# A new order of work at layer ends and at the start of two mixers of a transformer kernel

## Reference

```python
def swiglu(x, w13, w2):
    gate, up = jnp.split(x @ w13, 2, axis=-1)
    return (jax.nn.silu(gate) * up) @ w2
...
    idx_score = jnp.einsum('bqh,bqhk->bqk', wib, jax.nn.relu(dots))
...
    _, sel = lax.top_k(idx_score, topk)
...
    q = (rms_norm(cq, q_norm_g) @ w_uq).reshape(B, S, MLA_HEADS, MLA_NOPE + MLA_ROPE)
    kv = (rms_norm(ckv, kv_norm_g) @ w_ukv).reshape(B, S, MLA_HEADS, MLA_NOPE + MLA_V)
```

## Time and profile before

| | |
|---|---|
| Median of 3 runs | 2679.49 us (2677.05 to 2681.64) |
| The profiled execution | 2682.68 us, of which the span from first to last instruction is 2680.9 us |
| Mean granted TensorE clock | 0.971 |
| Busy share of the span: PE, PE weight load, DVE, ACT, POOL | 94%, 79%, 57%, 44%, 15% |
| DMA | 417.04 MB, 155 GB/s read from HBM over the span |
| Transfers of weights | 1 MB each, 48.1% of the time of 16 engines |

### The profile page before, as it was taken

The page is one execution under the profiler, slowest core; times in us unless marked ns, Lnnn a source line. Parts: engine busy times, 40 slices in busy tenths (PEclk is TensorE's granted clock), DMA queues, the critical chain, the costliest instruction groups (busy, mean ns, idle before and its releaser), DMA issues. The chain is left out here.

```text
span 2680.9 us, 32692 instructions
## 1 busy us (share of the span) xinstructions
PE 2527.9 (94%) x13229; PEld 2128.9 (79%) x13229; DVE 1524.4 (57%) x2152; ACT 1188.2 (44%) x1492; POOL 395.3 (15%) x466
## 2 busy tenths in 40 slices
PE   8998999999999999999789999998999987987998
PEld 6887878888888788888777888887778776886897
DVE  5546564464455544645455455456576565985455
ACT  4534454444444444444454444443444454333343
POOL 0001210000001000000220000002289112760000
PEclk9998999999999999999899999999999988988999
DMA  7554335555542555555135555554355531334453
GB/s 236 183 177 142 126 126 189 188 173 188 189 139 99 168 188 186 171 187 170 55 126 174 187 177 181 187 170 126 102 166 188 180 104 43 115 101 141 151 188 134
DMA packets 314967, 417.04 MB, mean 156 GB/s; under 512 B 18762, under 2 KB 273091, under 8 KB 314819
## 3 DMA queue, kind: packets, MB, share of 16 engines
q1 hardware_dynamic: 314818, 414.96, 48.1%
HBM read 413.87 MB, written 1.05 MB: 155 GB/s over the span
## 5 line engine op out<-in xcount | busy, mean ns | idle before, releaser
L456 DVE TENSOR_TENSOR wlo<-raw,whi 128x2048 fp32r<-128x2048 f32 (+3 forms) x402 | 919.7, 2293 | 640.3 <-ACT whi L448 639.4
L448 ACT ACTIVATE whi<-raw 128x2048 fp32r<-128x2048 f32 (+3 forms) x402 | 747.3, 1867 | 444.5 <-DMA raw<-in_ffn_w_dram 395.1
L569 PE MATMUL ps<-whi,xh 128*128 128x512 f32 (+4 forms) x2056 | 789.1, 384 | 25.7 <-DVE wlo L456 16.2
L570 PE MATMUL ps<-wlo,xh 128*128 128x512 f32 (+4 forms) x2056 | 777.5, 378 | 0.0
L571 PE MATMUL ps<-whi,xl 128*128 128x512 f32 (+4 forms) x2056 | 776.7, 378 | 0.0
L569 PEld LDWEIGHTS ps<-whi,xh 128*128 128x128 f32 x2056 | 397.7, 193 | 102.5 <-issue 23.3
L571 PEld LDWEIGHTS ps<-whi,xl 128*128 128x128 f32 x2056 | 397.2, 193 | 68.6
L570 PEld LDWEIGHTS ps<-wlo,xh 128*128 128x128 f32 x2056 | 398.2, 194 | 65.0
L569 PE MATMUL ps<-whi,oh 128*128 128x512 f32 x960 | 387.8, 404 | 6.0 <-DVE ol L1677 2.8
L571 PE MATMUL ps<-whi,ol 128*128 128x512 f32 x960 | 376.4, 392 | 0.0
L570 PE MATMUL ps<-wlo,oh 128*128 128x512 f32 x960 | 375.4, 391 | 0.0
(11 more groups left out here) (296 smaller groups left out, 2369.7 us busy)
## 6 DMA issues: line engine op xcount, KB each, us to landing
raw<-in_ffn_w_dram SPq DMA_DIRECT2D x352, 512.0 KB, 4.8
raw<-in_ffn_w_dram SPq DMA_DIRECT2D x88, 1024.0 KB, 5.0
raw<-in_w_ff_dram SPq DMA_DIRECT2D x32, 1024.0 KB, 5.3
raw<-in_w_out_dram SPq DMA_DIRECT2D x20, 1024.0 KB, 4.9
raw<-in_w_in_dram SPq DMA_DIRECT2D x20, 1024.0 KB, 5.2
raw<-in_dsa_w_in_dram SPq DMA_DIRECT2D x32, 512.0 KB, 4.4
raw<-in_dsa_w_in_dram SPq DMA_DIRECT2D x12, 1024.0 KB, 5.1
raw<-in_fox_w_in_dram SPq DMA_DIRECT2D x16, 512.0 KB, 4.4
```

The costliest lines, as they stand in the source:

```text
L448: act.activation(hi(u)[:, 0:w], raw[:, (slot[u] + 1) % SLOTS, 0:w], ACT.Copy).then_inc(sem("hi_ready"), 1)
L456: dve.tensor_tensor(lo(u)[:, 0:w], raw[:, (slot[u] + 1) % SLOTS, 0:w], hi(u)[:, 0:w].bitcast(F32), ALU.subtract).then_inc(sem("lo_ready"), 1)
L569: pe.matmul(o, ah, bh, start=start, stop=False, skip_group_check=True)
L570: pe.matmul(o, ah, bl, start=False, stop=False, skip_group_check=True)
```

## The change

Five things are moved. Nothing is added to or taken from the arithmetic.

1. **Pair 7, all four layers.** Six matmuls of the output projection that stood ahead of the transposes of pair 7 (`oproj(2, 1, 0)`) go to the start of `oproj`. Their place is taken by the second half of tile 1's residual and by six matmuls on the projection's first unit, which were the start of `oproj`. These are the last on that unit, so its slot is told free (`used`) inside the pair. A wait for the last mask (`masked`) is added ahead of them, since that half of tile 1 lies in bank 3, where scores were.
2. **The split behind it.** ScalarE splits the first unit of the coming `ffn` ahead of `outp(7)`, and the second one ahead of tile 0's normalization, not behind its transposes. VectorE splits the second unit between the two `xl` of tile 0, not behind both.
3. **First rows of the `ffn` w=1.** All of unit A(0)+1 runs ahead of the transposes of tile 1, which then stand between the two halves of tile 0's residual.
4. **Selecting mixer.** The projection of quad 1 (unit (1,0)) goes ahead of the transposes of pairs 0 and 1, and the other half of it (unit (1,1)) ahead of the scores of pair 0. The splits go forward by one place: (1,0) ahead of the index heads, and (1,2) ahead of the eight rounds of the selection. ScalarE copies the transposes of pair 0 to `qkT`, where VectorE did it.
5. **Latent mixer.** The values of heads 2 and 3 of the first quad go to bank 7, where they went to bank 2 and so waited until that was copied out; and VectorE copies the transposes of the next pair ahead of the two reciprocals, not behind them.

```diff
@@ -328,2 +328,6 @@
 
+        def kv_bank(q, j):
+
+            return 7 if q == 0 and j == 2 else 2
+
         def latent_bank(t, k):
@@ -843,5 +847,7 @@
                 if kind == "norm":
+                    if prev["kind"] == "oproj":
+                        split_hi(act, u + 1)
                     normal(0)
                     turned(0)
-                    if u < n_units and (ahead[u] == 2 or prev["kind"] == "oproj"):
+                    if u < n_units and ahead[u] == 2:
                         split_hi(act, u + 1)
@@ -891,3 +897,3 @@
                         act.activation(by_half(t), ps[:, t, :].rearrange("p (m c) -> p m c", m=2), ACT.Copy).then_inc(sem("ix_moved"), 1)
-                    split_hi(act, u + 2 + ahead[u])
+                    split_hi(act, u + 3 + ahead[u])
                     act.wait_ge(sem("ix_t"), 3 * n + 3)
@@ -896,3 +902,3 @@
                         if h == 4:
-                            split_hi(act, u + 3 + ahead[u])
+                            split_hi(act, u + 4 + ahead[u])
                         act.wait_ge(sem("ix_dots"), 8 * n + h + 1)
@@ -958,3 +964,3 @@
                             o = tm(q)[:, NT * 4 * MD:].rearrange("p (t h d) -> p t h d", t=NT, h=4)
-                            src = ps[:, 2, :].rearrange("p (t h d) -> p t h d", t=NT, h=2)[:, :, :, 0:DH]
+                            src = ps[:, kv_bank(q, j), :].rearrange("p (t h d) -> p t h d", t=NT, h=2)[:, :, :, 0:DH]
                             act.activation(o[:, :, 2 * j - 2:2 * j, 0:DH], src, ACT.Copy).then_inc(sem("qk_moved"), 1)
@@ -1008,2 +1014,6 @@
                         split_hi(act, u + 3 if col else unit_of(st, 1, 1))
+                        if st["mix"] == "dsa":
+                            split_hi(act, unit_of(st, 1, 2))
+                            act.wait_ge(sem("x_filled0"), b("x_filled0", 0) + 1)
+                            act.activation(qkT[:, 0, :], ps[:, 5, :], ACT.Copy).then_inc(sem("x_moved0"), 1)
                         turned_qk(1)
@@ -1041,6 +1051,6 @@
                             latents(q + 2, 0)
+                        if not col and i == NP - 1:
+                            split_hi(act, st["next"]["u"] + 1 + ahead[st["next"]["u"]])
                         outp(i)
 
-                if kind == "oproj":
-                    split_hi(act, u + 1 + ahead[u])
                 if kind == "oproj2":
@@ -1285,4 +1295,3 @@
                     if prev["kind"] == "oproj":
-                        turned(0)
-                        split_lo(dve, u + 1)
+                        turned(0, lambda: split_lo(dve, u + 1))
                         first_stats(1)
@@ -1343,2 +1352,3 @@
                     dve.tensor_copy(qkT[:, 0, :], ps[:, 5, :]).then_inc(sem("ix_k"), 1)
+                    split_lo(dve, u + 3 + ahead[u])
                     ch.wait()
@@ -1346,3 +1356,3 @@
                         if h == 4:
-                            split_lo(dve, u + 3 + ahead[u])
+                            split_lo(dve, u + 4 + ahead[u])
                         dve.wait_ge(sem("ix_relu"), 8 * n + h + 1)
@@ -1355,2 +1365,3 @@
                         last.then_inc(sem("ix_acc"), 1)
+                    split_lo(dve, u + 5 + ahead[u])
                     dve.wait_ge(sem("ix_acc"), 8 * n + 8)
@@ -1506,3 +1517,3 @@
                             dve.wait_ge(sem("av_done"), b("av_done", 0) + 4 * q - 4)
-                        src = ps[:, 2, :].rearrange("p (t h d) -> p t h d", t=NT, h=2)[:, :, :, DH:]
+                        src = ps[:, kv_bank(q, j), :].rearrange("p (t h d) -> p t h d", t=NT, h=2)[:, :, :, DH:]
                         dve.tensor_copy(v_tm[:, q % 2, :, 2 * j - 2:2 * j, :], src).then_inc(sem("v_moved"), 1)
@@ -1518,3 +1529,4 @@
                         split_lo(dve, u + 2 if col else unit_of(st, 1, 0))
-                        turned_qk(0)
+                        if st["mix"] != "dsa":
+                            turned_qk(0)
                         if not col:
@@ -1529,2 +1541,5 @@
                         q = i // 2
+                        if mla:
+                            for n in turns_at(st, i):
+                                turned_qk(n)
                         recip(2 * i)
@@ -1535,3 +1550,3 @@
                         for n in turns_at(st, i):
-                            if mla or n % 2 == 0:
+                            if not mla and n % 2 == 0:
                                 turned_qk(n)
@@ -1762,9 +1777,16 @@
                     unit_ready(pe, A(0) + 1)
-                    up(0, 1, 0, 0)
-                    turn_norm(prev, 1)
-                    for k in (1, 2, 3):
-                        last = up(0, 1, 0, k)
-                    last.then_inc(sem("h0_done"), 1)
-                    pe.wait_ge(sem("xt_dve"), b("xt_dve") - 1)
-                    residual(pe, b("cx_ready"), 0)
+                    if st["w"]:
+                        up(0, 1, 0).then_inc(sem("h0_done"), 1)
+                        residual(pe, b("cx_ready"), 0, range(4))
+                        turn_norm(prev, 1)
+                        pe.wait_ge(sem("xt_dve"), b("xt_dve") - 1)
+                        residual(pe, b("cx_ready"), 0, range(4, 8))
+                    else:
+                        up(0, 1, 0, 0)
+                        turn_norm(prev, 1)
+                        for k in (1, 2, 3):
+                            last = up(0, 1, 0, k)
+                        last.then_inc(sem("h0_done"), 1)
+                        pe.wait_ge(sem("xt_dve"), b("xt_dve") - 1)
+                        residual(pe, b("cx_ready"), 0)
                     for m in range(2):
@@ -1926,3 +1948,3 @@
                         unit_ready(pe, v)
-                        if q or j == 2:
+                        if q:
                             pe.wait_ge(sem("qk_moved"), b("qk_moved", 0) + 3 * q + (2 if j == 2 else 0))
@@ -1930,3 +1952,3 @@
                         for t in range(NT):
-                            last = token_major(pe, ps[:, 2, t * 256:(t + 1) * 256], v, 0, 256, t, range(2), 256, k0=3)
+                            last = token_major(pe, ps[:, kv_bank(q, j), t * 256:(t + 1) * 256], v, 0, 256, t, range(2), 256, k0=3)
                         used(last)
@@ -2120,11 +2142,16 @@
                             last.then_inc(sem("fg_cum"), 1)
+                        if st["mix"] == "dsa":
+                            wide(1, 0, 0)
+                            wide(1, 0, 1)
                         turn(0)
                         turn(1)
-                        wide(1, 0, 0)
-                        wide(1, 0, 1)
                         if st["mix"] == "fox":
+                            wide(1, 0, 0)
+                            wide(1, 0, 1)
                             pe.wait_ge(sem("fg_sel"), 1)
-                        scores(0)
+                            scores(0)
                         wide(1, 1, 0)
                         wide(1, 1, 1)
+                        if st["mix"] == "dsa":
+                            scores(0)
                     for i in range(NP):
@@ -2144,3 +2171,6 @@
                             if i == 7:
-                                oproj(2, 1, 0)
+                                pe.wait_ge(sem("masked"), b("masked", 0) + NH)
+                                residual(pe, b("cx_ready"), 1, range(4, 8))
+                                oproj(0, 0, 1, [1])
+                                used(oproj(0, 1, 1, [1]))
                             pturn(i)
@@ -2245,5 +2278,3 @@
 
-                    residual(pe, b("cx_ready"), 1, range(4, 8))
-                    piece(0, 0, 1, [1])
-                    used(piece(0, 1, 1, [1]))
+                    piece(2, 1, 0)
                     by_columns(lambda c, ns: piece(3, c, 0, ns)).then_inc(sem("y0_done"), 1)
```

## The result

| | before | changed |
|---|---|---|
| Median (lowest to highest, 4 runs each) | 2678.27 us (2672.71 to 2681.64) | 2656.45 us (2654.45 to 2659.97) |
| The profiled execution, its span | 2682.68, 2680.9 | 2659.97, 2658.2 |
| Mean granted clock | 0.971 | 0.975 |

What follows compares the result with a forecast made beforehand. TensorE was taken to bound the kernel: its work, 153 us idle and its clock. Gains of 10.2 (ends), 7.2 (selecting mixers) and 4.7 (latent mixer) sum to 22.1 us, taking the median from 2679.49 to 2657.4, range 2650 to 2666.

Steps and rivals of the forecast that it cites:

- Layer ends: Four layer ends, parts 1 to 3: 2.55 us gained per end, 10.2 us in all, bounds 1.2 to 3.9 per end.
- The start T: Layer end 0: start of tile 1's first transposes, forecast 1.5 us earlier, at some 370.4 on the old kernel's clock.
- The waits behind it: Layer end, behind tile 1's first transposes: waits for `cx` 0.3, the residual's second half 0.55, `xl` 1.1, `gt` 1.05 us.
- the clock fall in half of the cases: Layer ends: clock falls behind the four short waits in half of the cases, costing 0.7 us net per end.
- the wait of 2.25 is gone: Layer ends: TensorE's 2.25 us wait for tile 1's normalization goes, as more matmuls and transposes run ahead of it.
- The slower rival: Layer ends: late load of A(0)+1 holds up ScalarE's split and tile 0's normalization; about 2685 us, chance 0.05.
- Selecting mixers: Layers 0 and 3, part 4: scores of pair 1 start earlier; 4.2 and 3.0 us gained, 7.2 in sum, bounds 0 to 10.3.
- Latent mixer: Layer 2, part 5: other bank and earlier `qkT` copy shorten two waits; 4.7 us gained, bounds 0 to 6.8.
- 1.3 given back: Latent mixer: losses of 0.55 us for GpSimd's late rotation and 0.75 for the later reciprocals.
- 0.8 for the low part: Latent mixer: some 0.8 us of the first wait, 2.78, stays because the unit's low part must be there.
- The rival of the clock falls: Layer ends and three mixers: clock falls behind several short waits; gain only 15.6 us, median 2663.9, chance 0.16.

## Why the prediction was right

**Layer ends: right place, a wrong account of what pays.** The start T came at 366.3 for 366.2, which is a coincidence. The prediction took T from `xn`. But `xn` was ready at 365.5, 2.2 us earlier than before where 1.5 had been counted, and TensorE came 0.8 us behind it by its own work. The waits behind it were forecast as 0.3, 0.55, 1.1 and 1.05, together 3.0, and measured 0, 0.39, 0.87 and 0.84, together 2.1: each was a little less, so the gain was undersized. I had the clock fall in half of the cases. It fell in none: at the 12 ends of the old form in the profiles of this study the clock has a low stretch that begins within or behind the wait of 2.25, at the 40 ends of the ten kernels with part 1 none. These two together would make a gain of 4.06 + 1.8 - 2.1 = 3.8 per end; measured were 3.0. The other 0.8 is not idle time by the profile but longer busy time. Of it 0.46 comes with the new first rows, since it goes when they are undone: two groups of four transposes take 0.66 each there, eight in one piece 1.04. The rest is open; the ends of matmuls are modelled.

What failed is the sentence that the wait of 2.25 is gone because TensorE "now has all 12 and four transposes of the residual" to run ahead. (Before, it had three matmuls of A(0)+1 there and not two, as the timeline from 368.79 on shows.) Without these rows the wait is 1.81, with a clock of 1.00, and the end is 0.7 us shorter. The end hung on VectorE's and ScalarE's chain for tile 1 (statistics, `xn`, transposes, `xl`, `gt`), and `xn` in it came 2.2 us earlier. Parts 1 and 2 carry the gain, and only together: the ends lose 15.4 us without part 1 and 10.8 without part 2, and part 1 pays by the load that it starts early.

**The slower rival** was priced from the issue to the landing: free up to 10 us, decisive from 17 us. The measured landing was 351.48 behind an issue at 346.16, 5.3 us, so no cost, as forecast. But its price was too low: the run without part 1 had its landing 10.0 us behind the changed kernel's issue, which by my count was still free, and lost up to 5.0 us at an end. I had counted to the time at which ScalarE is wanted for `xn`, and not taken off the split's own 1.9; and I had not counted the eight transposes and ten matmuls that then run at the lower clock.

**Selecting mixers: right by its steps.** 4.2 and 3.0 forecast, 4.25 and 3.17 measured in the profiled execution, and in the mean over all profiles with the old form (three) and the changed one (seven) 4.5 and 2.9. The starts of the selection, of the masks and of the scores of pair 1 were each within 0.5 us. That the selection's start sets the end was shown by both runs that moved it: with the selection 3.8 and 3.3 us earlier, the scores of pair 1 came 3.5 and 3.4 earlier (each profile's own shift taken off). In these means idle time is 1.5 us less in layer 0 and 2.5 in layer 3, and the low clock is 4.7 and 0.5 us shorter. So about half of layer 0's gain is the clock's, and nearly all of layer 3's is idle time.

**Latent mixer: right in sum, wrong in its parts.** Forecast was idle time of 2.5, clock 3.5, and 1.3 given back. Idle time saved is 4.2: the first wait went completely, where I had left 0.8 for the low part, and the second lost 1.3 where I had said 0.5. The 0.8 was no error. Three of the ten profiles with both halves do have that wait, of 0.64, 0.90 and 0.96; here it is in the run without part 3:

```profile
1294.15 0.39 PE L573 MATMUL ps<-whi,xh 128*128 128x256 f32 x1 [0.90 <-DVE wlo L460]
```

In these three the low stretch behind the wait of 2.37 ahead of it is 3.4 us long. In the other seven it is 6.8, TensorE is slower up to there, and it comes when the low part is ready. The clock gave nothing in the profile of the changed kernel (20.5 us of low clock before and after). In the mean of the ten, idle time is 2.8 us less than before and the low clock 6.0 us shorter, and the mixer is 4.9 us shorter, against a forecast of 4.7.

**The rival of the clock falls.** At the layer ends the new order has transposes in groups of four, eight and four with short waits between, some 3.5 us in which TensorE runs no other matmul (365.7 to 369.24), and the clock is 1.00 in the window. The rule of the Trainium skill ("TensorE: Matmul & The Clock Gate", Part 4 "PE-mode transpose"), that transposes don't count as busy for the clock in the way of matmuls, would have had it fall. The trace doesn't agree: at none of the 36 ends with this order (nine kernels) was there a low stretch at or behind these groups.

**What cancelled.** The ends gave 1.6 more than forecast, the selecting mixers 0.2 more, the latent mixer 0.4 less; places with unchanged code gave 1.6 and took 2.4. That the forecast was within 1 us of the median is partly luck: one term's error was covered by another's, and the median of the kernel before alone lay between 2678.3 and 2681.7 in the five comparisons made.

## What to carry to other kernels

When an engine waits for a chain on other engines, giving it more work ahead of the wait hid the wait here but didn't move what comes behind: look at what the chain itself waits for (here a load's slot, a split in front of the statistics), and move that. An order that lets a transfer start earlier may be what makes all the other moves possible, so undo the parts one by one before keeping them: of three at the layer ends one started the load, one used it, and one cost time.

Read idle time and granted clock apart, for the same stretch, in several profiles. A single pair of profiles differs by steps of 1.6 us in places that nobody touched.

## What was not expected of the hardware

Whether an unchanged mixer with 1.0 us of idle time gets 3.4, 6.8 or 10.2 us of low clock changes from run to run (58.3, 59.9 and 61.5 us). Behind a single wait of 1.81 (eight ends), or waits of 1.34, 0.49, 0.39, 0.86 and 0.82 within 15 us (four ends), the clock stayed at 1.00, while it fell at all 12 ends with 1.34 and 2.25 some 3 us apart. Whether it takes both of these isn't shown: in the run without part 1 it fell in or behind single waits of 2.68, 3.49 and 2.32, and stayed at 1.00 with one of 2.57.
